# Hybrid attention: a head pair's sink, reciprocal, gates and scaling moved to the head of the next slot

## The reference, cut to what matters

```python
def hybrid_layer(...):
    o_a = banded_attention(q_a, k_a, v_a, A_WINDOW, attn_sinks)      # 4 heads, softmax over keys and a sink
    o_b = nsa_mixer(...)     # 4 heads, 3 softmaxes each: compressed keys, selected keys, window
    o_c = gated_delta_net(cqkv, ca, cb, cz, ...)                     # 4 heads of 128
    x = x + gt_m * (jnp.concatenate([o_a, o_b, o_c], axis=-1) @ w_out)
    ...
# A: p = softmax([s, sink])[:-1]
# B: o = gates[0] * o_cmp + gates[1] * o_slc + gates[2] * o_win
# C, per chunk of 64 tokens, after a triangular solve has made u and w:
def step(state, inp):
    v_new = u_c - w_c @ state
    o_c = qd_c @ state + qk_c @ v_new
    state = state * gl_c + kd_c.T @ v_new
```

## Time and profile before

| | |
|---|---|
| time, median of 3 runs | 2819.03 us (2815.92 to 2820.66) |
| span of the profiled execution | 2817.7 us |
| PE busy | 2697.4 us, 96% of the span |
| DVE, ACT busy | 1627.0 us (58%), 1122.5 us (40%) |
| slots 0 to 31, first hybrid layer | 1499 to 1640 us |
| slots 0 to 31, second hybrid layer | 2242 to 2383 us |

### The profile page before, as it was taken

One profiled execution on the slowest core, in us unless ns is written; L12 is line 12 of the kernel. 1 busy time (PEld: TensorE's weight loads), 2 busy tenths in 40 slices (PEclk: granted clock), 3 DMA queues, 4 the chain that ended last, 5 costly groups with the idle time before them and its releaser, 6 DMA issues.

```text
span 2817.7 us, 41838 instructions
## 1 busy us (share of the span) xinstructions
PE 2697.4 (96%) x17282; PEld 2122.8 (75%) x17282; DVE 1627.0 (58%) x2917; ACT 1122.5 (40%) x1964; POOL 9.4 (0%) x21
## 2 busy tenths in 40 slices
PE   6999999999999999999998899999999988999998
PEld 4777888867666788886876667888878766788886
DVE  6588746573555875667456765444465577533334
ACT  2544324234555442323345553222334466422222
POOL 0000000000000000000000000000000000000000
PEclk9999999999999999999999999999999999999999
DMA  6435555533222365563330013444433200222222
GB/s 255 139 134 181 189 186 174 188 115 108 74 69 64 108 209 190 189 198 120 102 123 17 3 57 124 140 144 148 139 120 104 98 3 3 90 97 97 97 97 82
DMA packets 92093, 336.42 MB, mean 119 GB/s; under 512 B 10480, under 2 KB 10736, under 8 KB 91776
## 3 DMA queue, kind: packets, MB, share of 16 engines
q1 hardware_dynamic: 86800, 315.40, 34.3%
q10 hardware_dynamic: 3792, 14.11, 1.4%
q0 software_dynamic: 1312, 4.23, 0.5%
HBM read 331.57 MB, written 2.13 MB: 118 GB/s over the span
## 4 chain that ended last, share of the span: by engine, by line
PE 46%; ACT 4%; DVE 3%; issue 1%; DVEq 0%; ACTq 0%
PE bank L649 12%; PE bank L650 12%; PE bank L651 12%; ACT probs L2291 1%; PE bank L931 1%; PE bank L916 1%; PE bank L1016 1%; PE bank L902 1%; PE bank L692 0%; PE bank L693 0%; PE bank L694 0%; PE bank L989 0%; PE bank L1190 0%; PE bank L1004 0%; DVE probs L1638 0%
## 5 line engine op out<-in xcount | busy, mean ns | idle before, releaser
L1295 DVE TENSOR_TENSOR weights_low<-weight_ring,weights_high 128x1024 fp32r<-128x1024 f32 x404 | 493.8, 1224 | 425.4 <-ACT weights_high L2046 425.3
L649 PE MATMUL bank<-in_high,weights_high 128*128 128x512 f32 x1848 | 731.1, 396 | 7.6 <-DVE in_low L1444 3.5
L651 PE MATMUL bank<-in_high,weights_low 128*128 128x512 f32 x1848 | 720.6, 390 | 0.0
L650 PE MATMUL bank<-in_low,weights_high 128*128 128x512 f32 x1848 | 720.5, 390 | 0.0
L2046 ACT ACTIVATE weights_high<-weight_ring 128x1024 fp32r<-128x1024 f32 x404 | 424.4, 1051 | 442.5 <-PE bank L651 301.8
L649 PEld LDWEIGHTS bank<-in_high,weights_high 128*128 128x128 f32 x1848 | 347.6, 188 | 93.9 <-issue 8.6
L650 PEld LDWEIGHTS bank<-in_low,weights_high 128*128 128x128 f32 x1848 | 347.8, 188 | 73.7 <-issue 3.4
L651 PEld LDWEIGHTS bank<-in_high,weights_low 128*128 128x128 f32 x1848 | 347.6, 188 | 73.2
L649 PE MATMUL bank<-hidden_split,weights_high 128*128 128x512 f32 x864 | 336.9, 390 | 0.0
L651 PE MATMUL bank<-hidden_split,weights_low 128*128 128x512 f32 x864 | 336.1, 389 | 0.0
L650 PE MATMUL bank<-hidden_split,weights_high 128*128 128x512 f32 x864 | 336.1, 389 | 0.0
(11 more groups left out here) (390 smaller groups left out, 3328.2 us busy)
## 6 DMA issues: line engine op xcount, KB each, us to landing
weight_ring<-stream SPq DMA_DIRECT2D x597, 512.0 KB, 3.5
mixer_out<-cmp ACTq DMA_DIRECT2D x6, 1024.0 KB, 4.9
hidden<-forget_rows POOLq DMA_DIRECT2D x16, 256.0 KB, 3.7
residual<-x ACTq DMA_DIRECT2D x4, 512.0 KB, 12.3
mixer_out<-cmp SPq DMA_DIRECT2D x2, 1024.0 KB, 6.6
out<-mixer_out ACTq DMA_DIRECT2D x4, 512.0 KB, 2.8
constants<-consts ACTq DMA_DIRECT2D x1, 1821.5 KB, 20.3
silu_c<-c ACTq DMA_DIRECT2D x2, 512.0 KB, 4.3
```

Of the source, the lines that this page charges most:

```text
L649: pe.matmul(bank[:, :], WHI[:, z, cols], high, start=(k == 0), stop=False)
L650: pe.matmul(bank[:, :], WHI[:, z, cols], low, start=False, stop=False)
L651: ins = pe.matmul(bank[:, :], WLO[:, z, cols], high, start=False, stop=(k == ktiles - 1))
L1295: v.tensor_tensor(WLO[:, z, :], ring[:, n % RING, :], WHI[:, z, :].bitcast(F32), ALU.subtract).then_inc(*mark("weights_low", "low", n))
```

## The change

Of pair `d-1`, the normalisation moves from slot `d-1` to the head of slot `d`, on DVE and on ACT. This is for the hybrid layers only (`next_slot`); the other attention of the program, `fox`, keeps its order. PE's program isn't changed. A wait for DVE's own last instruction is added ahead of the two additions of `kv`, since the normalisation, with its own waits, no longer stands between the scaling of the state (L1984) and the addition (L1996).

```diff
+    next_slot = lambda name: name[0] == "hyb"
...
         def paired_attention(name, items, probs, turn_banks, slots, bias, fill, end):     # DVE
...
             for d in range(slots):
                 c = 8 * (d % 4)
+                if next_slot(name) and 1 <= d <= n:
+                    normalise(d - 1)
                 if d < n:
...
                 fill(d, 0)
-                if d < n:
-                    it, tot = items[2 * d], COL[:, c + 2:c + 4]
...
+                if d < n and not next_slot(name):
+                    normalise(d)
                 fill(d, 1)
...
                 if c < 7:
                     after_c = state[(c + 1) % 2]
+                    v.wait_ge(*last(sem))
                     v.wait_ge(*at("scan_kv", l, c))
...
         def paired_attention(name, items, probs, turn_banks, slots, fill, end):           # ACT
...
                 if early:
                     fill(d, 0)
+                if next_slot(name) and 1 <= d <= n and scalar_scales(name, items[2 * d - 1]):
+                    normalise(d - 1)
                 if d < n:
...
-                if d < n and scalar_scales(name, items[2 * d + 1]):
-                    i = 2 * d + 1
-                    p = probs[i % 4][:, 0:items[i]["width"]]
-                    s.wait_ge(*at(*name, "scales", d))
-                    s.activation(p, p, ACT.Copy, scale=COL[:, c + 3:c + 4]).then_inc(*mark(sem, *name, "probs", i))
+                if d < n and not next_slot(name) and scalar_scales(name, items[2 * d + 1]):
+                    normalise(d)
                 fill(d, 1)
```

More of the change, by code:

```diff
@@ L1627, in paired_attention, with normalise @@
             n, sem = len(items) // 2, "vector_attention"
+            def normalise(d):
+                c = 8 * (d % 4)
+                it, tot = items[2 * d], COL[:, c + 2:c + 4]
+                if it.get("sink") is not None:
+                    v.wait_ge(*at(*name, "sink", 2 * d + 1))
+                    v.tensor_tensor(tot, tot, COL[:, c + 4:c + 6], ALU.add).then_inc(*step(sem))
+                    v.wait_ge(*last(sem))
+                else:
+                    v.wait_ge(*at(*name, "exp", 2 * d + 1))
+                gated = it.get("gates") is not None
+                v.reciprocal(tot, tot).then_inc(*(step(sem) if gated else mark(sem, *name, "scales", d)))
+                v.wait_ge(*last(sem))
+                if gated:
+                    v.tensor_tensor(tot, tot, it["gates"], ALU.mult).then_inc(*mark(sem, *name, "scales", d))
+                    v.wait_ge(*last(sem))
+                for z in range(1 if scalar_scales(name, it) else 2):
+                    i, t1 = 2 * d + z, COL[:, c + 2 + z:c + 3 + z]
+                    it, p = items[i], probs[i % 4][:, 0:items[i]["width"]]
+                    if it.get("valid") is not None:
+                        v.scalar_tensor_tensor(p, p, t1, it["valid"], ALU.mult, ALU.mult).then_inc(
+                            *mark(sem, *name, "probs", i))
+                    else:
+                        v.tensor_scalar(p, p, t1, None, ALU.mult).then_inc(*mark(sem, *name, "probs", i))
             for d in range(slots):
                 c = 8 * (d % 4)
+                if next_slot(name) and 1 <= d <= n:
+                    normalise(d - 1)
                 if d < n:
@@ L2280, in paired_attention, with normalise @@
             n, sem = len(items) // 2, "scalar_attention"
+            def normalise(d):
+                c, i = 8 * (d % 4), 2 * d + 1
+                p = probs[i % 4][:, 0:items[i]["width"]]
+                s.wait_ge(*at(*name, "scales", d))
+                s.activation(p, p, ACT.Copy, scale=COL[:, c + 3:c + 4]).then_inc(*mark(sem, *name, "probs", i))
             for d in range(slots):
```

## The result

| | before | after |
|---|---|---|
| time, median | 2818.39 us (2815.92 to 2821.94, 12 runs) | 2825.12 us (2819.96 to 2828.74, 12 runs) |
| span of the profiled execution | 2817.7 us | 2825.6 us |
| ratio of after to before | | 1.0023, 95% interval 1.0015 to 1.0032 |

The kernel after is slower by 6.7 us, and the interval excludes 1 (the line of 0.2% that the prediction's chances use lies inside it). 2826.5 was predicted. The sum is near, but the reasons are only half right, as the experiments show: by an estimate from profiles, the order itself costs about 2.6 us, and falls of TensorE's granted clock make the rest.

A forecast was written before the change was run, and what follows sets the result against it. PE was taken as the bound, busy 96% and idle some 38 us in both stages. 2817.7 + 6.7 (order) + 1.0 (clock) = 2825.4 us of span; the median 1.3 above gives 2826.7, said as 2826.5; range 2811 to 2836.

The forecast's parts named there:

- the prediction's walk: Slots followed in the new order, delaying PE's second turn: 3.35 us a layer, 6.7 in both; chance 0.50.
- What bounds the kernel: PE, busy 96%; of DVE's 13.8 us of exp and sink waits a layer, only 4.0 us of PE waits stand behind.
- The head of the slot: Normalisation (0.67 us) ahead of the max: 1.05 us from second turn to max, 0.19 more in slot 6, landing on PE.
- ACT's scaling ahead of the exp: Where ACT copies a p before the exps, the scaling (0.51 us at 256 wide) joins that chain; elsewhere it costs nothing.
- The clock: TensorE's granted clock may fall in the first layer's slots 15 and 16 too: between 0 and 2 us, taken as +1.
- The added wait: DVE's wait for L1984 ahead of the kv additions, 7 slots a layer: 0, as kv comes later; upper bound 1.5 us.
- The scan: Slots 24 to 31, DVE nearly full: +0.15 us a layer, some slots waiting for kv and others gaining as much.
- The end: Last pair's max 0.7 us later, but the scaling no longer ahead of the output copies: +0.15 us a layer.
- Faster: Rival: the exp waits were on the path and PE gets back 4.0 us a layer: 2811 us; chance 0.20.
- No change: Rival: PE's 18 us of idleness in a layer take up the shifts: 2819 us; chance 0.18.
- Much slower: Rival: each of the 23 delta slots pays about 0.4 us, 9.2 a layer, never given back: 2837 us; chance 0.12.

The follow-up runs named there:

- e12: The kernel after with 3 idle matmuls of 128 columns, which nothing reads, ahead of each xt: 2817.27 us, ratio 1.0002.
- e1: The kernel after with DVE's normalisation back at its old place, so only ACT's scaling moves: 2820.89 us, ratio 1.0009.
- e6: The kernel before with the normalisation moved for pairs 12 to 23 only: 2816.24 us in one execution, 2817.39 us (0.9998) timed in rounds.
- e7: The kernel before with the normalisation moved for pairs 24 to 31 only, the scan: 2818.0 us in one execution.
- e3: The kernel before with many idle matmuls, 6 ahead of xt and 3 ahead of the second turn in 13 slots: 2824.07 us, ratio 1.0020.
- e4: The kernel after with many idle matmuls, 6 ahead of xt and 3 ahead of the second turn in 13 slots: 2825.51 us, ratio 1.0026.
- e9: The kernel before with 3 idle matmuls ahead of each xt and 3 ahead of the second turn in slots 8 and 10: 2818.51 us, ratio 0.9998.

## Why the prediction was right, and where only by luck

How late the max of a slot starts, counted from slot 0, against the kernel before (us, first layer; worked out from the maxes' starts in the timelines):

| slot | 4 | 6 | 11 | 12 | 17 | 23 | 28 | 31 |
|---|---|---|---|---|---|---|---|---|
| after | 0.8 | 2.1 | 2.6 | 5.0 | 5.2 | 5.5 | 5.7 | 6.4 |
| e12, the same order at full clock | 0.8 | 0.2 | 0.8 | 0.6 | 0.8 | 1.1 | 1.3 | 2.0 |
| the prediction's walk (without clock) | 0.8 to 0.9 | | 1.4 | | 2.0 | 3.05 | | 3.2 |

Some 0.7 us of slot 31 is only the normalisation that now stands ahead of the max and not behind it; behind the last max the stage takes 17.0 us in e12 and 17.8 in before without a fall. After and e12 are 4.4 us apart in slot 12 and 4.4 in slot 31: the two falls make the whole difference.

**What bounds the kernel**, and that the exp waits aren't PE's: right. All 13.8 us of them went, and PE got nothing of it. Only the small things on ACT came back. (The 1.32 us of slot 6 is the longest of the sink waits and not the second longest; nothing hangs on it.)

**The head of the slot**: right, and to 0.02 us where PE ran at full clock. Slots 5 and 6 of after:

```profile
1531.12 0.33 PE L932 MATMUL bank<-constants,probs 128*128 128x128 f32 x1
1531.26 0.42 DVE L1971 TENSOR_TENSOR work<-work,bank 128x256 f32<-128x256 f32 x1 [1.11 <-PE bank L1203]
...
1532.78 0.48 DVE L1665 CUSTOM_DVE_ANT_0 probs<-bank,constants,columns 128x256 f32<-128x256 f32 x1
...
1535.72 0.41 PE L932 MATMUL bank<-constants,hidden 128*128 128x128 f32 x2 [1.05 <-ACT probs_T L2319]
1536.17 0.42 DVE L1676 COPY probs_T<-bank 128x256 f32<-128x256 f32 x1 [0.69 <-PE bank L932]
1536.51 0.15 DVE L1635 TENSOR_TENSOR columns<-columns 128x2 f32<-128x2 f32 x1
1536.69 0.17 DVE L1640 RECIPROCAL columns<-columns 128x2 f32<-128x2 f32 x1
1536.89 0.35 DVE L1652 TENSOR_SCALAR probs<-probs,columns 128x256 f32<-128x256 f32 x1
...
1537.16 0.48 DVE L1665 CUSTOM_DVE_ANT_0 probs<-bank,constants,columns 128x256 f32<-128x256 f32 x1
```

Slot 6's turn ends at 1536.13 and the max of slot 7 starts at 1537.16, 1.03 us behind, where 1.05 was predicted. In slot 6 the max is 1.33 behind the turn (1531.45 to 1532.78), since DVE's `q` had waited 1.11 us for matmuls at half clock. Normalisation, start to next start, takes 0.65 (1536.51 to 1537.16), 0.67 predicted. The second turn's wait grew, as said.

**ACT's scaling ahead of the exp**: its place is right. Slot 19, whose scaling is 512 wide, was to lose 0.7 us; in e12 the max of slot 20 is 0.7 later than that of slot 19, and 0.6 in e1, where only ACT's part moved. In the measured total ACT's move is the smaller part (e1: 2.5 us in both layers, with an interval that touches 0), but by the estimate under e1 it is most of what the order costs at full clock.

**The walk, 3.35 us a layer: mis-sized.** Slots 0 to 4 were right (0.8). From slot 5 on it was wrong: at full clock the delay doesn't grow to 1.4, 2.0 and 3.05, but goes back to 0.2 in slots 5 to 7 and then stands at 0.3 to 1.3 up to slot 28. In the walk's own measure, the end of PE's second turn, it is less still: in e12 0.3 in slot 11, 0.3 in slot 17 and 0.8 in slot 23 of the first layer. This is what the prediction itself named as its weakness, that engines catch up in the slots taken as late throughout. The walk had taken the `q` that starts a microsecond earlier as worth nothing, because its consumer stands behind the second turn. One place shows that it can be worth something: the first `p` behind slot 5's second turn waits 0.28 us for DVE's `q` in before (1529.32), and in e12 it doesn't wait and starts 0.3 us earlier, counted from slot 0. That this is what gives back most of the head's cost over the other slots is not shown. For the price of the order I need before at full clock, which no run had in a whole stage. As an estimate: 137.2 us from first to last max in its first layer, whose one fall there is free, and 17.8 for the tail in its second layer, where the clock stayed up in it (19.4 in the first), make 155.0. The second layer gives the same: 156.6 less the 1.5 us of its fall at slots 15 to 17. e12's 156.2 and 156.4 are 1.2 and 1.4 more: 2.6 us for both layers instead of 6.7. Two stages without any idle matmuls bear out the size, the second ones of e6 and e7, whose only fall is the free one at slot 5: 155.9 and 155.5 us, so 0.9 for pairs 12 to 23 and 0.5 for pairs 24 to 31. Against it stand e3 and e4, 4.5 us, with 51 idle matmuls in each stage; why they differ more is not shown. e12's own idle matmuls are in its stages, but of their 1.8 us a layer 1.5 lies in a wait that was there anyway: `xt`'s for DVE went from 2.5 to 1.0 us.

**The clock, +1.0 in all: mis-sized, and misplaced.** The prediction saw the falls of the earlier trace rows and that the first layer might get the second's fall in slots 15 and 16. It took the fall at slot 5 as given, and didn't ask whether the same order change would make it longer. After at 160.6 and 160.4 less e12 at 156.2 and 156.4 is 4.4 + 4.0 = 8.4 us of clock. Before has falls of its own, 156.6 - 155.0 = 1.6 a layer. So the account of the two profiled spans is: order 2.6, clock 8.4 - 3.2 = 5.2, together the 7.8 that the stages differ by. (That they add up is no check, since both terms are counted from the same 155.0; if that is off, what one gains the other loses.) The prediction's 6.7 + 1.0 = 7.7 was the right sum of two wrong terms: that it hit 2826.5 to 1.4 us is luck. The twelve runs of after bear the clock out too, if roughly: the quickest, 2819.96 us, had a mean granted clock of 0.996, the four over 2827 had 0.992 or 0.993 (and so had some between).

The Trainium skill, "TensorE: Matmul & The Clock Gate", Part 1, says that the clock follows how busy the engine has been and drops to half after idleness. The rows agree in kind: PE had been busy 0.77 and 1.01 of 2 us each ahead of the fall to 0.50. Neither this nor the rows of before told which of two such stretches would fall longer, and here 1.8 us of idle matmuls in each layer were worth about what the change had cost, 6.7 us in both.

**The added wait, 0**: right. In the scan of after DVE waits ahead of the addition (L2004) three times, 0.8 us, and each time for PE's `kv`. One of them, slot 28:

```profile
1632.45 0.69 DVE L1991 TENSOR_TENSOR work<-work,columns 128x512 f32<-128x512 f32 x1
1633.39 0.76 DVE L2004 TENSOR_TENSOR work<-work,bank 128x256 f32<-128x256 f32 x2 [0.26 <-PE bank L1259]
```

The scaling ends at 1633.14, `kv` later, so the wait for one's own last instruction is covered. In the other four slots another instruction of DVE stands between, and the addition starts between 0.09 us ahead of its end and 0.09 behind. The upper bound of 1.5 us was far off. **The scan**, +0.15: in e12 0.2 from the max of slot 23 to that of slot 28, but 0.7 to that of slot 30 in the first layer and 0.5 in the second, so somewhat low. **The end**, +0.15: the stretch behind the last max is 0.8 us shorter (17.0 against 17.8), which takes back the lateness of that max.

**The rivals.** Faster is out, since PE got none of the exp waits back. No change is out for this kernel, whose interval excludes 1, but of the order alone it was nearer to the truth than its 0.18 said: with six small idle matmuls a layer the changed kernel is at 2817.27 against 2817.55. Much slower is out.

## What to carry to other kernels

A wait on an engine that isn't the bound is worth nothing until a wait on the bound is shown to end with it; moving work from behind one wait to ahead of a chain's first step costs there what it saves elsewhere. In a stage where the bounding engine idles in short pieces, compare its busy time, not only its idle time, before and after: if the same matmuls take longer, the clock is the term, and it can be the largest. A few idle matmuls ahead of a wait that is there anyway are a cheap test for it; they are worth keeping only where that test shows a fall. And before a fall is put down to an order, look whether it is there in both layers and in other profiles of the same instructions: here one at slots 15 to 17 was not.

## What the runs showed of the hardware that I had not expected

- A fall of the granted clock can be free or dear by where it comes and how long it lasts: before's at slot 5 cost nothing to 0.1 us (against e9), after's at slot 10 cost 2.4 us (max of slot 11 to slot 12), because it met `last` and `uw`, 1.97 us instead of 1.15 and 4.2 instead of 2.4.
- Six idle matmuls (1.8 us) in a stage of 157 us removed two falls of the clock in each layer, which had lasted some 14 us together (e12). The second of them had begun at 1550 us, some 30 us behind the nearest place where idle matmuls were put.
- Where the clock falls can differ between executions of the same instructions: the fall at slots 15 to 17 is in the second layer of before and not in its first, and in the first layer of e7 and not in its second. So that e9, the order of before with idle matmuls, had a fall there doesn't show that the order or the idle matmuls made it.
